# Order of the first loads, split first weights, idle products at the start, GpSimd adds between the layers, and last tiles by token halves

## The chip, the cores and the metric

The kernel runs on one core of one Trainium2 chip. The metric is the device time of one execution in microseconds (us); the time before is the median of three runs.

## The reference

Two transformer-like blocks are applied to 512 tokens of width 1024, everything in float32. The first block is a mixer of three branches and an MLP; the second has two layers of three sub-blocks each. Cut to what matters here:

```python
# first block
u = rms_norm(x, g_mix); z = u @ w_in              # the first product is the slice "v" of w_in
...                                               # three branches, merge, h = h + y @ w_o, MLP
h = rms_norm(h, g_final)
# second block, for each layer l of 2
def post_add(x, y, i, res_w):
    return x + res_w * mod[:, i, 2] * rms_norm(y, norm_post[l, i])
x = post_add(x, swiglu(pre(x, 0), ffn_w_in[l, 0], ffn_w_out[l, 0]), 0, 0.5)
x = post_add(x, token_mixer(pre(x, 1), ...), 1, 1.0)
x = post_add(x, swiglu(pre(x, 2), ffn_w_in[l, 1], ffn_w_out[l, 1]), 2, 0.5)
```

`pre` is an RMS norm with a scale and a shift for each feature. Both norms need, for each token, a sum of squares over all 1024 features, which lie on partitions and in 8 tiles.

## The kernel before, in words

A tensor of 1024 features by 512 tokens is held as 8 tiles of 128 partitions x 512 tokens: `hT` is the running state, `Y` (`YT`) the output of a sub-block, `XH` and `XL` the normed input as a high and a low part. Every float32 product is made of three: high weights by high input, low weights by high input, and high weights by low input. ScalarE rounds a weight block to its high part (`hi`, L1339: `wh<-w`), VectorE subtracts it to get the low part (`lo`, L2024: `wl<-w,wh`). All weights come through three slots of 1 MB (`wslots`), loaded by SyncE in the order of the stages (`load` inside the `sync` block, L496). A block's slot is free (`w_free`) once its `lo` is done. `plan` lists the stages, their blocks `s.b`, their output tiles `s.o`, the PSUM bank of each, and which `hi`/`lo` of a later block is done ahead of which tile (`s.ahead`).

The order of each engine's work is written out by hand, engine by engine; each instruction counts up its engine's semaphore, and `at(name)` is the count another engine waits for.

The start: SyncE issues four pieces of x (each 2 tiles, 512 KB), the constants `cf`, the parameters `pr`, the bf16 constants (`BIG<-in_cb`), and then weight blocks. ScalarE squares the 8 tiles of x (L1405), VectorE adds them in a tree (L1976), TensorE sums over partitions by products with a constant column (`token_sums`, L725), ScalarE takes the root (L1371), VectorE the reciprocal, and TensorE spreads the four columns of factors over a PSUM bank (`spread`, L752). VectorE then makes the normed tile k (`feed`, L2066), ScalarE its high part (`high`, L1401), and TensorE starts stage `v` (`four_tiles`, L610): for each k, 8 products of 128x512 on four output tiles; the 32 products with `XL` follow. Product k=4 needs the second weight block of `v`.

The links: after a sub-block, `link` forms both norms at once. TensorE makes the sums and two spreads, then 8 idle products (`warm`, L732). VectorE then goes through the tiles in a pipeline: `scaled(k)` (L2490, Y times gain and factor, the factor in PSUM bank 4), `added(k)` (L2496, hT = hT + Y, all in SBUF), `normed(k)` (L2502, the next norm, its factor in PSUM bank 2). ScalarE makes `XH` of tile k (L1703), and TensorE takes it in `four_tiles` (L610 or L612). Five links have such an addition; the link from the first block (`final`) has none. Where the next stage is `u` (two links), VectorE also makes the low part of a weight block in two halves (`lo_half`, L2032), the second one ahead of the wait for the first spread.

GpSimd (`POOL`) has the sums of the dots (`y_adds`, L3016) and low parts in the FFNs (L2998). It is idle in the part of the link described.

The end: the last stage is `("out", 3, 2)` with four weight blocks of two output tiles each, 6 x 3 products of 128x512 a tile. VectorE adds a finished tile to `Y` (L2780), ScalarE squares it (L1722), GpSimd gathers. After the last tile, `last_link` (TensorE) and `last_post` (VectorE) make the norm and the last addition: 8 times `scaled` (L2525) and 8 times `added` (L2529), and SyncE stores a tile of `hT` as soon as it is done (L545).

Of the kernel before, what the change touches and what calls it, by code (L numbers as in the profile page):

```python
# [9 lines left out]
F32 = mybir.dt.float32  # L10
# [13 lines left out]
CF = {}  # L24
# [54 lines left out]


# [53 lines left out]
_T = [("j", 0)] * 3  # L134

# [108 lines left out]
def program(nc, A, out, marks_in):  # L244
# [4 lines left out]
    with ctx:  # L249
# [54 lines left out]
        x_landed = [sem(f"x_landed{i}") for i in range(4)]  # L304
        const_landed, w2_landed, rg_landed, mem_landed, xo_landed, c_landed = [sem(n) for n in (
# [29 lines left out]
        def last_mm(name):  # L335
            return at("mm", st_of[name].o[-1][-1])

# [145 lines left out]
        def _(sp):  # L483
            for i in range(4):
                sp.dma_start(hT[:, 2 * i:2 * i + 2, :], A["x"].rearrange("p (k t) -> p k t", k=8)[:, 2 * i:2 * i + 2]).then_inc(
                    x_landed[i], 16)
            sp.dma_start(cf[:, :], A["cf"]).then_inc(const_landed, 16)
            sp.dma_start(pr[:, :], A["pr"]).then_inc(const_landed, 16)
            sp.dma_start(BIG[:, 0:NCB], A["cb"]).then_inc(const_landed, 16)
            ticks, mod_end = 0, MOD_FIRST  # L490

            def load(s, g):
                b = s.b[g]
                if b >= 3:
# [48 lines left out]
            for k in range(8):  # L543
                sp.wait_ge(*at("h_new", (1, 2), k))
                sp.dma_start(out[:, 512 * k:512 * k + 512], hT[:, k, :]).then_inc(out_landed, 16)  # L545
            sp.wait_ge(*at("bar", "end", "dve"))
            sp.wait_ge(*at("bar", "end", "pool"))
            sp.wait_ge(out_landed, 128)

        @block.tensor  # L550
        def _(pe):
# [50 lines left out]
            def four_tiles(s, xh, xl, xw):  # L602
# [13 lines left out]
                for k in range(8):  # L616
                    pe.wait_ge(*xw("h", k))
                    for t in range(4):
                        if (k, t) == (0, 0):
                            pe.wait_ge(*at("lo", s.b[0]))  # L620
# [25 lines left out]
            def gemm(s, xh, xl=None, xw=None):  # L646
# [7 lines left out]
                for g, b in enumerate(s.b):  # L654
                    if s.four and g < 2:
                        continue
                    if s.raw:
# [57 lines left out]

            def run(s, xh, xl=None, xw=None, after=None):
# [54 lines left out]
            run(st_of["v"], XH, XL, xw("mix"))  # L771
            run(st_of["g"], XH, XL)
# [320 lines left out]
            def last_link(r):  # L1093
                pe.wait_ge(*at("y_acc", r))
                token_sums(banks[3], tmps[4], 512, True, False)
                pe.wait_ge(*at("y_sq", r, 7))
                token_sums(banks[3], tmps[2], 512, False, True).then_inc(*TE.up(("sq_mm", ("y", r), 7)))
                warm(3)
                spread(("y", r), 512)

            def ffn(l, f):
# [15 lines left out]
                if r == (1, 2):  # L1117
                    last_link(r)
# [208 lines left out]
        def _(act):  # L1327
# [22 lines left out]
            def evict(s, fn, ahead=True):  # L1350
                for g, b in enumerate(s.b):
                    for t, o in enumerate(s.o[g]):
# [50 lines left out]
            for k in range(8):  # L1403
                act.wait_ge(x_landed[k // 2], 16)
                actf(tmps[k][:, :], hT[:, k, :], ACT.Square).then_inc(*AC.up(("sq", "mix", k)))  # L1405
            act.wait_ge(const_landed, 48)
            first_root()
            root("mix", 512)
            hi(st_of["v"], 0)
# [304 lines left out]
            def last_square(r, j, wait):  # L1714

                t = tmps[4] if j == 0 else tmps[2] if j == 7 else tmps[j % 2]
# [3 lines left out]
                if 3 <= j < 7:  # L1720
                    act.wait_ge(*at("y_add", r, j - 2))
                actf(t[:, :], Y[:, j, :], ACT.Square).then_inc(*AC.up(("y_sq", r, j)))  # L1722

# [62 lines left out]
            def ffn(l, f):  # L1786
# [30 lines left out]
                if r == (1, 2):  # L1817
                    root(("y", r), 512)
# [142 lines left out]
        def _(dve):  # L1961
# [8 lines left out]
            for m in (1, 2, 4):  # L1970
                for k in range(0, 8, 2 * m):
                    if m == 1:
                        dve.wait_ge(*at("sq", "mix", k + 1))
                    elif k == 0:
                        own()
                    tt(tmps[k][:, :], tmps[k][:, :], tmps[k + m][:, :], ALU.add).then_inc(*DV.up(("x_sq",)))  # L1976
            dve.wait_ge(const_landed, 48)
            v.tensor_copy(cb_[:, :], BIG[:, 0:NCB]).then_inc(*DV.up(("cb",)))
# [56 lines left out]
            def evict(s, fn, ahead=True):  # L2035
                for g, b in enumerate(s.b):
                    for t, o in enumerate(s.o[g]):
# [47 lines left out]
            lo(st_of["v"], 0)  # L2085
            dve.wait_ge(*at("spread", "mix"))
            feed("mix", lambda k: p("g_mix", k), norm_low("mix"), HIGH_FIRST[0:4])
            lo(st_of["v"], 1)
            feed("mix", lambda k: p("g_mix", k), norm_low("mix"), HIGH_FIRST[4:8] + [("l", k) for k in LOWS])
            run(st_of["v"])  # L2090
# [358 lines left out]
            def link(r, nxt):  # L2449
# [31 lines left out]
                if nxt[1] == 1:  # L2481
                    lo_half(st_of[("u", nxt[0])], 1, 1)
# [10 lines left out]
                def added(k):  # L2493
                    if not final:
                        dve.wait_ge(*at("y_scaled", r, k))
                        tt(hT[:, k, :], hT[:, k, :], Y[:, k, :], ALU.add).then_inc(*DV.up(("h_new", r, k)))  # L2496

# [9 lines left out]
                added(0)  # L2507
                for k in range(8):
# [3 lines left out]
                    if k < 7:  # L2512
                        added(k + 1)
# [6 lines left out]
            def last_post(r):  # L2520
                gc = newc(168)
                rms(("y", r), 512)
                for k in range(9):
                    if k < 8:
# [732 lines left out]
```

## Time and profile before

| what | us |
|---|---|
| median of 3 runs (3423.95 to 3426.64) | 3424.88 |
| the profiled execution's own time | 3428.77 |
| its span | 3427.0 |
| TensorE busy (PE, 98%) | 3352.0 |
| VectorE busy (DVE, 49%) | 1673.1 |
| ScalarE busy (ACT, 36%) | 1224.2 |
| GpSimd busy (POOL, 13%) | 435.4 |

The profile has engines in columns: PE is TensorE's products, PEld its weight loads, DVE VectorE, ACT ScalarE, POOL GpSimd, SP SyncE. A float32 product that isn't of the rounded kind shows as two records. "L705" is a line of the kernel; the arrow points from inputs to the output tile.

### The profile page before, as it was taken

What the parts mean: (1) busy time and instruction counts of PE and PEld (TensorE: products, weight loads), DVE (VectorE), ACT (ScalarE), POOL (GpSimd) and SP (SyncE); (2) the same over time, 40 slices, a digit from 0 to 9 for tenths busy, and PEclk for the clock granted to TensorE, in tenths of its full rate; (3) what the DMA queues carried; (4) which work ended last, traced back from release to release, by engine and by line L of the source; (5) the groups of instructions that cost most, each with busy time, mean ns of one, the idle gap of its engine ahead of it and who ended that gap; (6) DMA issues with size and microseconds to landing.
All of it is one profiled execution on the core that took longest, in us unless ns stands there. A gap on an engine that the chain in (4) does not pass through costs nothing.

```text
span 3427.0 us, 38703 instructions
## 1 busy us (share of the span) xinstructions
PE 3352.0 (98%) x16102; PEld 2640.4 (77%) x16110; DVE 1673.1 (49%) x2190; ACT 1224.2 (36%) x1770; POOL 435.4 (13%) x338
## 2 busy tenths in 40 slices
PE   8999999999999999999999999999999999999998
PEld 6755477788888888888588888878888876888886
DVE  5555666453335635664335534575457533452233
ACT  3374466332223232224533322233223245342222
POOL 0100013122220100112011100110101210210001
PEclk9999999999999999999999999999999999999999
DMA  5412643243333333223032344433431322222221
GB/s 192 148 44 81 185 172 131 109 148 142 140 143 119 107 138 137 75 111 117 21 121 99 135 143 146 135 115 111 152 105 68 124 92 68 86 86 99 99 95 53
DMA packets 78351, 393.40 MB, mean 115 GB/s; under 512 B 8416, under 2 KB 17120, under 8 KB 45024
## 3 DMA queue, kind: packets, MB, share of 16 engines
q1 hardware_dynamic: 66048, 370.41, 30.9%
q10 hardware_dynamic: 12128, 20.52, 1.7%
q8 instruction: 127, 2.08, 0.2%
q14 instruction: 48, 0.39, 0.0%
HBM read 372.02 MB, written 18.87 MB: 114 GB/s over the span
## 4 chain that ended last, share of the span: by engine, by line
PE 91%; DVE 4%; ACT 3%; issue 2%; DMA 0%; ACTq 0%; POOL 0%; SPq 0%; DVEq 0%; POOLq 0%
PE pb L705 22%; PE pb L707 21%; PE pb L706 21%; PE pb L612 3%; PE pb L673 2%; PE pb L674 2%; PE pb L610 2%; PE pb L681 2%; PE pb L876 1%; PE pb L894 1%; PE pb L855 1%; ACT wh L1339 1%; DVE wl L2024 1%; PE pb L1211 1%; PE pb L1161 1%
## 5 line engine op out<-in xcount | busy, mean ns | idle before, releaser
L2024 DVE TENSOR_TENSOR wl<-w,wh 128x2048 fp32r<-128x2048 f32 (+3 forms) x264 | 582.8, 2207 | 889.0 <-ACT wh L1339 886.6
L705 PE MATMUL pb<-XH,wh 128*128 128x512 f32 (+1 forms) x2488 | 985.0, 396 | 2.4 <-DVE wl L2024 1.6
L707 PE MATMUL pb<-XH,wl 128*128 128x512 f32 (+1 forms) x2488 | 970.9, 390 | 0.0
L706 PE MATMUL pb<-XL,wh 128*128 128x512 f32 (+1 forms) x2488 | 970.1, 390 | 0.0
L1339 ACT ACTIVATE wh<-w 128x2048 fp32r<-128x2048 f32 (+3 forms) x264 | 471.7, 1787 | 284.5 <-PE pb L707 188.3
L705 PEld LDWEIGHTS pb<-XH,wh 128*128 128x128 f32 (+1 forms) x2488 | 466.5, 188 | 108.6 <-issue 8.2
L706 PEld LDWEIGHTS pb<-XL,wh 128*128 128x128 f32 (+1 forms) x2488 | 466.5, 187 | 101.7 <-issue 4.6
L707 PEld LDWEIGHTS pb<-XH,wl 128*128 128x128 f32 (+1 forms) x2488 | 465.9, 187 | 100.9
L2998 POOL TENSOR_TENSOR HL<-tmps,HH 128x512 fp32r<-128x512 f32 x120 | 165.6, 1383 | 1312.3 <-ACT HH L1661 1312.3
L705 PE MATMUL pb<-HH,wh 128*128 128x512 f32 x768 | 303.0, 394 | 2.3 <-DVE YT L2780 2.3
L706 PE MATMUL pb<-HL,wh 128*128 128x512 f32 x768 | 301.1, 392 | 0.0
L707 PE MATMUL pb<-HH,wl 128*128 128x512 f32 x768 | 301.1, 392 | 0.0
L2011 DVE CUSTOM_DVE_ANT_0 mreg<-mreg,pr 128x1024 f32<-128x1024 f32 x144 | 187.1, 1300 | 39.0 <-DMA mreg<-in_mod_w 38.8
L1661 ACT ACTIVATE HH<-tmps 128x512 fp32r<-128x512 f32 x120 | 75.4, 631 | 347.9 <-DVE tmps L2771 329.9
L705 PEld LDWEIGHTS pb<-HH,wh 128*128 128x128 f32 x768 | 145.9, 190 | 33.7 <-DVE YT L2780 3.7
L707 PEld LDWEIGHTS pb<-HH,wl 128*128 128x128 f32 x768 | 145.6, 190 | 30.8
L706 PEld LDWEIGHTS pb<-HL,wh 128*128 128x128 f32 x768 | 145.9, 190 | 30.1
L1797 ACT ACTIVATE tmps<-pb 128x512 f32<-128x512 f32 x88 | 52.4, 598 | 307.5 <-PE pb L707 281.7
L2771 DVE TENSOR_TENSOR tmps<-tmps,pb 128x512 f32<-128x512 f32 x88 | 60.3, 687 | 185.6 <-PE pb L707 181.4
L673 PE MATMUL pb<-HH,wh 128*128 128x512 f32 x256 | 99.6, 389 | 0.0
L674 PE MATMUL pb<-HH,wl 128*128 128x512 f32 x256 | 99.6, 389 | 0.0
L2780 DVE TENSOR_TENSOR YT<-YT,pb 128x512 f32<-128x512 f32 x64 | 43.8, 685 | 111.7 <-PE pb L707 86.0
(479 smaller groups left out, 4057.8 us busy)
## 6 DMA issues: line engine op xcount, KB each, us to landing
w<-in_f_in SPq DMA_DIRECT2D x88, 1024.0 KB, 4.8
mreg<-in_mod_w SPq DMA_DIRECT2D x144, 512.0 KB, 3.6
w<-in_f_out SPq DMA_DIRECT2D x32, 1024.0 KB, 5.0
w<-in_w_up SPq DMA_DIRECT2D x16, 1024.0 KB, 5.7
w<-in_w_dn SPq DMA_DIRECT2D x16, 1024.0 KB, 5.7
w<-in_m_g SPq DMA_DIRECT2D x16, 1024.0 KB, 4.8
w<-in_f_out SPq DMA_DIRECT2D x16, 768.0 KB, 4.2
w<-in_w_rm SPq DMA_DIRECT2D x8, 1024.0 KB, 5.7
```

The lines of the kernel that those rows point to most:

```text
L610: return mm(dst, tokens(s, x, k, t), slot(s, k // 4)[part][:, 512 * (k % 4):512 * (k % 4) + 512], **kw)
L612: return mm(dst, slot(s, t // 2)[part][:, at_:at_ + 128], x[:, k, :], **kw)
L673: mm(dst, hi[:, cs], xh[:, k, :], start=k == 0, stop=False)
L674: mm(dst, lo[:, cs], xh[:, k, :], start=False, stop=False)
L705: mm(dst, hi[:, cs], xh[:, k, :], start=k == 0, stop=False)
L706: mm(dst, hi[:, cs], xl[:, k, :], start=False, stop=False)
L707: x = mm(dst, lo[:, cs], xh[:, k, :], start=False, stop=fin)
L1339: actf(slot(s, g)[0][:, 0:s.cols], wslots[b % 3][:, 0:s.cols], ACT.Copy).then_inc(*AC.up(("hi", b)))
L1661: actf(HH[:, j, :], t, ACT.Copy).then_inc(*AC.up(("hh", *name, j)))
L2011: v.tensor_tensor_reduce(out=mslots[t % 2], in0=mslots[t % 2], in1=csil, scale=1.0, scalar=p("mod_b", t), op0=ALU.mult, op1=ALU.add, accum ...
L2024: tt(low[:, 0:s.cols], wslots[b % 3][:, 0:s.cols], h[:, 0:s.cols].bitcast(F32), ALU.subtract).then_inc(*DV.up(("lo", b), ("w_free", b)))
L2998: tt(HL[:, j, :], t, HH[:, j, :].bitcast(F32), ALU.subtract).then_inc(*PO.up(("hl", *name, j)))
```

## The change

What it does, in five parts; the diff is cut to the code that carries them.

1. Loads and first weights. The constants `cf` are loaded in three pieces: the identity (128 columns) and the last 17 columns after the first piece of x, the middle one (1409 columns) with the bf16 constants behind the second weight block. The first weight block of `v` comes in two halves of 512 KB with semaphores of their own, ahead of `pr`; ScalarE and VectorE split it half by half. `four_tiles` waits for the first half at k=0 and for the whole at k=2.
2. First norm. ScalarE takes a root of a dummy first and squares 7 tiles, VectorE squares the eighth. The tree is replaced by three groups (tiles 0-3, 4-5, 6-7), each summed over tokens by its own four products.
3. Idle products. GpSimd clears `cb_` at once; TensorE runs 24 idle products of 128x512 on it, then waits for the constants and the first sums.
4. Links. The additions k = 1 to 7 go to GpSimd (`h_adds`), k = 0 stays; the second `lo_half` moves behind `normed(1)` and `scaled(3)`.
5. End. Output tiles 4 to 7 of the last stage are computed for tokens 0-255 and then for tokens 256-511 (`half_tiles`), 144 products of 128x256 in place of 72 of 128x512. Sums, root, reciprocal, spread, scaling, addition and store follow for each half, the first half's sums and spread between the products of the second; additions are shared by VectorE and GpSimd. There are 16 stores in place of 8.

```diff
@@ sync
+            front, tail = CF["ropeC"][0], CF["padmax"][0]
             for i in range(4):
                 sp.dma_start(hT[:, 2 * i:2 * i + 2, :], ...).then_inc(x_landed[i], 16)
-            sp.dma_start(cf[:, :], A["cf"]).then_inc(const_landed, 16)
-            sp.dma_start(pr[:, :], A["pr"]).then_inc(const_landed, 16)
-            sp.dma_start(BIG[:, 0:NCB], A["cb"]).then_inc(const_landed, 16)
+                if i == 0:
+                    sp.dma_start(cf[:, 0:front], A["cf"][:, 0:front]).then_inc(first_landed, 16)
+                    sp.dma_start(cf[:, tail:NCF], A["cf"][:, tail:NCF]).then_inc(first_landed, 16)
...
+                if b == 0:
+                    sp.dma_start(wslots[0][:, 0:1024], s.srcs[0][:, 0:1024]).then_inc(half_landed, 16)
+                    sp.dma_start(wslots[0][:, 1024:2048], s.srcs[0][:, 1024:2048]).then_inc(w_landed[0], 16)
+                    sp.dma_start(pr[:, :], A["pr"]).then_inc(pr_landed, 16)
+                    return
...
+                if b == 1:
+                    sp.dma_start(cf[:, front:tail], A["cf"][:, front:tail]).then_inc(const_landed, 16)
+                    sp.dma_start(BIG[:, 0:NCB], A["cb"]).then_inc(const_landed, 16)
@@ tensor
+            def half_tiles(s, xh, xl, between):
+                for n, (half, j) in enumerate(HALF_TILES):       # (0,4..7), (1,4..7)
+                    g, t = j // 2, j % 2
+                    if half == 0 and t == 0:
+                        pe.wait_ge(*at("lo", s.b[g]))
+                    if n < 2:
+                        bank_free(s, s.o[g][t])
+                    else:
+                        pe.wait_ge(*at("ev_half", s.name, *HALF_TILES[n - 2]))
+                    for k in range(kts):                          # three products of 128x256
...
+                        if (half, j, k) in between:
+                            between[half, j, k]()
...
-            pe.wait_ge(const_landed, 48)
-            pe.wait_ge(*at("x_sq"))
-            token_sums(banks[3], tmps[0], 512, True, True).then_inc(*TE.up(("sq_mm", "mix", 7)))
+            pe.wait_ge(*at("cb_zero"))
+            warm(24)
+            pe.wait_ge(first_landed, 32)
+            pe.wait_ge(*at("x_sum", 3))
+            token_sums(banks[3], tmps[0], 512, True, False)
+            pe.wait_ge(*at("x_sum", 5))
+            token_sums(banks[3], tmps[4], 512, False, False)
+            pe.wait_ge(*at("x_sum", 7))
+            token_sums(banks[3], tmps[6], 512, False, True).then_inc(*TE.up(("sq_mm", "mix", 7)))
...
-                    last_link(r)
+                    half_tiles(st_of[("out", i, 2)], HH, HL, {(1, 4, 3): lambda: last_sums(r, 0), (1, 5, 1): lambda: last_spread(0)})
+                    last_sums(r, 1)
+                    warm(2)
+                    last_spread(1)
@@ vector, link
-                if nxt[1] == 1:
-                    lo_half(st_of[("u", nxt[0])], 1, 1)
                 dve.wait_ge(*at("spread", name))
...
                 for k in range(8):
                     normed(k)
                     if k < 6:
                         scaled(k + 2)
-                    if k < 7:
-                        added(k + 1)
+                    if k == 1 and nxt[1] == 1:
+                        lo_half(st_of[("u", nxt[0])], 1, 1)
@@ vector, last_post
+                for j in range(4, 8):
+                    add_y(0, j)
+                add_y(1, 4)
+                inverse(0)
+                dve.wait_ge(*at("last_spread", 0))
+                scaled(0, 0, 1, 2)
+                add_y(1, 5)
+                scaled(0, 3, 4)
+                added(0, 3)
+                add_y(1, 6)
+                scaled(0, 5, 6, 7)
+                added(0, 4)
+                add_y(1, 7)
+                inverse(1)
+                dve.wait_ge(*at("last_spread", 1))
+                scaled(1, 0, 1)
+                for k in (2, 4, 6):
+                    scaled(1, k)
+                    added(1, k - 1)
+                    scaled(1, k + 1)
+                added(1, 7)
@@ gpsimd
+            gp.memset(cb_[:, :], 0.0).then_inc(*PO.up(("cb_zero",)))
...
+            def h_adds(r):
+                for k in range(1, 8):
+                    pool.wait_ge(*at("y_scaled", r, k))
+                    tt(hT[:, k, :], hT[:, k, :], Y[:, k, :], ALU.add).then_inc(*PO.up(("h_new", r, k)))
+            # last_adds: gathered(0, 4..6), gathered(1, 4), added(0, 0), gathered(1, 5), added(0, 1, 2),
+            #            gathered(1, 6), added(0, 5, 6, 7), added(1, 0, 2, 4, 6)
```

## Rows read from the trace of the kernel before

**Rows 1.** The profile's first lines: span, and busy time of TensorE's products and others.

```profile
span 3427.0 us, 38703 instructions
PE 3352.0 (98%) x16102; PEld 2640.4 (77%) x16110; DVE 1673.1 (49%) x2190; ACT 1224.2 (36%) x1770; POOL 435.4 (13%) x338
```

**Rows 2.** Timeline, first 45 us: start, duration, engine, line, operation, count [idle before].

```profile
7.50 2.43 ACT L1405 ACTIVATE tmps<-hT 128x512 f32<-128x512 f32 x4 [0.44 <-DMA hT<-in_x]
12.86 1.83 PE L725 MATMUL pb<-cf,tmps 128*128 128x1 f32 x8 [12.86 <-DVE tmps L1976]
15.26 2.08 PE L752 MATMUL pb<-cf,rcol 128*128 128x128 f32 x8 [0.56 <-DVE rcol L2084]
20.70 0.80 PE L610 MATMUL pb<-wh,XH 128*128 128x512 f32 x1 [3.36 <-ACT XH L1401]
22.53 1.90 ACT L1339 ACTIVATE wh<-w 128x2048 fp32r<-128x2048 f32 x1
24.46 2.29 DVE L2024 TENSOR_TENSOR wl<-w,wh 128x2048 fp32r<-128x2048 f32 x1 [2.50 <-ACT wh L1339]
26.78 2.72 DVE L2066 SCALAR_TENSOR_TENSOR tmps<-hT,pr,pb 128x512 f32<-128x512 f32 x4
37.13 7.42 PE L610 MATMUL pb<-wh,XL 128*128 128x512 f32 x32
```

**Rows 3.** Busy time by stretch: stretch, PE, PEld, DVE, ACT, POOL (records), granted clock, DMA.

```profile
20.70:24.20 3.50, 3.50 (x8) 2.82 (x9) 1.26 (x2) 3.45 (x4) 0.00 (x0) 1.00 0.92 379
1871.30:1873.00 1.70, 1.70 (x9) 1.70 (x9) 0.52 (x4) 0.30 (x1) 0.00 (x0) 0.50 0.96 402
```

**Rows 4.** DMA issues of the first 40 us: KB each, median us to landing.

```profile
BIG<-in_cb SPq DMA_DIRECT2D x1, 256.0 KB, 8.3
```

**Rows 5.** Timeline of one link into an FFN, VectorE and TensorE.

```profile
1875.15 0.75 DVE L2502 SCALAR_TENSOR_TENSOR tmps<-hT,cols,pb 128x512 f32<-128x512 f32 x1
1877.20 0.75 DVE L2502 SCALAR_TENSOR_TENSOR tmps<-hT,cols,pb 128x512 f32<-128x512 f32 x1
1876.97 0.47 PE L612 MATMUL pb<-XH,wh_extra 128*128 128x512 f32 x1 [0.53 <-ACT XH L1703]
1892.76 0.62 PE L612 MATMUL pb<-XL,wh_extra 128*128 128x512 f32 x2
```

**Rows 6.** Timeline of one link into stage `u`.

```profile
1465.94 1.20 DVE L2032 TENSOR_TENSOR wl<-w,wh 128x1024 fp32r<-128x1024 f32 x1
1470.97 0.60 PE L610 MATMUL pb<-wh,XH 128*128 128x512 f32 x1 [0.77 <-ACT XH L1703]
1486.97 7.68 PE L610 MATMUL pb<-wh,XL 128*128 128x512 f32 x32
```

**Rows 7.** Timeline of GpSimd and of VectorE beside it, at two places.

```profile
1508.40 1.30 POOL L3045 TENSOR_TENSOR tmps<-tmps 128x512 f32<-128x512 f32 x1 [20.63 <-DVE tmps L2819]
1508.77 0.68 DVE L2821 TENSOR_TENSOR tmps<-pb,BIG 128x512 f32<-128x512 f32 x1
2238.51 1.28 DVE L2011 CUSTOM_DVE_ANT_0 mreg<-mreg,pr 128x1024 f32<-128x1024 f32 x1
2238.67 2.25 POOL L3016 TENSOR_TENSOR tmps<-tmps 128x512 f32<-128x512 f32 x1 [5.36 <-DVE tmps L2446]
```

**Rows 8.** Timeline of TensorE in the compression products (two records to a product).

```profile
158.76 5.19 PE L811 MATMUL pb<-tmps,w 128*128 128x124 f32 x45
```

**Rows 9.** Timeline of the end.

```profile
3394.95 1.76 DVE L2024 TENSOR_TENSOR wl<-w,wh 128x1536 fp32r<-128x1536 f32 x1 [2.08 <-ACT wh L1339]
3408.08 0.39 PE L707 MATMUL pb<-HH,wl 128*128 128x512 f32 x1
3409.91 1.29 PE L725 MATMUL pb<-cf,tmps 128*128 128x1 f32 x8 [0.66 <-ACT tmps L1722]
3412.29 1.87 PE L752 MATMUL pb<-cf,rcol 128*128 128x128 f32 x8
3423.09 1.29 DVE L2529 TENSOR_TENSOR hT<-hT,YT 128x512 f32<-128x512 f32 x2
```

More of the change, by code:

```diff
@@ L134 @@
 _T = [("j", 0)] * 3
+HALF_TILES = [(half, j) for half in range(2) for j in range(4, 8)]
 def _steps(what, a, b):
@@ L336, in last_mm, with hs, half_bank @@
             return at("mm", st_of[name].o[-1][-1])
+        def hs(half):
+            return slice(256 * half, 256 * half + 256)
+        def half_bank(s, n):
+            return banks[s.bank[s.o[2][n % 2]]]
         def newc(i, n=8):
@@ L619, in four_tiles @@
                         if (k, t) == (0, 0):
+                            pe.wait_ge(*at("lo_half" if s.name == "v" else "lo", s.b[0]))
+                        if (k, t) == (2, 0) and s.name == "v":
                             pe.wait_ge(*at("lo", s.b[0]))
@@ L1817, in ffn @@
                 if r == (1, 2):
-                    root(("y", r), 512)
+                    for more in st_of[("out", i, 2)].ahead[2, 0]:
+                        hi(*more)
+                    for half, j in HALF_TILES:
+                        last_half(r, j, half)
+                        if (half, j) == (1, 4):
+                            last_root(0)
+                    last_root(1)
                 else:
@@ L2506, in link @@
                 scaled(1)
-                added(0)
+                if not final:
+                    dve.wait_ge(*at("y_scaled", r, 0))
+                    tt(hT[:, 0, :], hT[:, 0, :], Y[:, 0, :], ALU.add).then_inc(*DV.up(("h_new", r, 0)))
                 for k in range(8):
@@ new lines, in add_y, with inverse @@
+                def add_y(half, j):
+                    dve.wait_ge(*at("mm_half", st_last.name, half, j))
+                    tt(Y[:, j, hs(half)], Y[:, j, hs(half)], half_bank(st_last, j)[:, hs(half)], ALU.add).then_inc(
+                        *DV.up(("ev_half", st_last.name, half, j)))
+                def inverse(half):
+                    cs = slice(2 * half, 2 * half + 2)
+                    dve.wait_ge(*at("last_root", half))
+                    v.reciprocal(rcol[:, cs], rcol[:, cs]).then_inc(*DV.up(("last_inverse", half)))
@@ new lines, in scaled, with added @@
+                def scaled(half, *ks):
+                    for k in ks:
+                        stt(out=Y[:, k, hs(half)], in0=Y[:, k, hs(half)], scalar=gc[:, k:k + 1], in1=banks[4][:, hs(half)],
+                            op0=ALU.mult, op1=ALU.mult).then_inc(*DV.up(("y_scaled", r, k, half)))
+                def added(half, *ks):
+                    for k in ks:
+                        dve.wait_ge(*at("y_scaled", r, k, half))
+                        tt(hT[:, k, hs(half)], hT[:, k, hs(half)], Y[:, k, hs(half)], ALU.add).then_inc(
+                            *DV.up(("h_new", r, k, half)))
@@ new lines, in last_post @@
+                for more in st_last.ahead[2, 0]:
+                    lo(*more)
+                for j in range(4, 8):
+                    add_y(0, j)
+                own()
+                add_y(1, 4)
[8 more added lines that the diff above has]
+                added(0, 4)
@@ L3062, in _ @@
                 y_adds(r)
+                h_adds(r)
                 ffn(l, 1)
```

169 lines of the change are left out of this document (123 added, 46 removed).

## The prediction

> **What bounds the kernel now.** Read the first lines first: TensorE's products fill 3352 of 3427 us [rows 1]. So nothing that only relieves another engine can pay; what is left are the 75 us in which TensorE has no product, and products that run at the lower clock. The waits by engine say where: 12.9 us before the first sum, 3.4 us before the first product of stage `v`, about 1 us inside each link, and the timeline shows some 18 us behind the last product. The change touches just these, so each is worked out from its timeline, as a chain: what is the last thing that its end waits for. Sums are made in the profiled execution (its own time 3428.77, span 3427.0), which is 3.9 above the median of 3424.88; I carry the difference over to the median.
>
> **The start.** The chain before: last piece of x there at about 8.7 (the last two squares end at 9.93, 0.62 each), the tree of adds, eight records of sums from 12.86 to 14.7, root and reciprocal until 15.26, spread until 17.3, low part of the first block on VectorE until 19.2, normed tile and high part, first product 20.70; the `XL` products start at 37.13 [rows 2]. TensorE and VectorE both stood in front of the constants too: the last of them landed at 3.71 + 8.3 = 12.0 [rows 4].
>
> After, step by step. The two small pieces of `cf` go ahead of x's second to fourth piece. By bytes that is 73 KB at the 3.45 MB that had landed by 12.0, 0.2 us; I take 0.4 and keep 1.2 as the upper end, for 256 short descriptors and two more issues in SP's queue. The last x is there at 9.1. ScalarE squares 7 of 8 and VectorE the eighth; then one add: the last group is ready at 11.1 (an add is 0.69 long and they follow at 0.60, [rows 9]; the second group's add, from 9.1, and VectorE's square stand in front of it). Four products of sums: 0.9 at the full clock (as the 1.29 and less of [rows 9] tell, partly slow), 1.83 at the low one [rows 2]; I take 1.4, to 12.5. Root, reciprocal and their gaps took 15.26 - 14.69 = 0.6: 13.1. Spread 0.9 to 2.08; I take 1.7: 14.8. In its shadow go the first half of `hi` (about 1.0 of 1.90) before the root, and half of `lo` (1.20, [rows 6]) between reciprocal and spread. `pr` has about as many bytes in front of it as before the last constant, so 12.2: hidden. Normed tile 0.7 and high part 0.65 and the first product starts at 16.2, 4.5 earlier.
>
> But the gain is not read there. Product k=4 wants the second weight block, whose `hi` stands behind `high(3)` on ScalarE and whose `lo` stands ahead of `normed(4)` on VectorE. That chain: 14.8, two normed tiles 1.35, half a `lo` 1.2, two normed tiles 1.35, high part 0.7, `hi` 1.90, `lo` 2.29, normed tile 0.7, high part 0.7 [rows 2]: 25.1. TensorE, with 32 products at 0.227, would be there at 23.5, or at 25.2 if 8 of them run at the low clock (3.5 us for 8, [rows 3]). So an early clock is worth little here: at 25.1 VectorE's chain takes the place of the clock. Before, k=4 began at 37.13 - 32 x 0.227 = 29.9 (from the pace inside the 7.42 of [rows 2]). Gain 4.8 at most, I take 4.7. With everything at the full clock it is 5.6; with sums and spread at the low clock and the loads late, 3.
>
> The 24 idle products (about 8 slow ones at 0.43, then 16 fast ones at 0.22) end between 8 and 10, so they are over before the last group is ready. Their good is the clock of sums and spread, 0.9 and 0.8 us, and that is not sure: in a link the granted clock was at half (0.50, the 1.2 GHz level) from 1871.3, after a stretch in which TensorE had run small products and hardly a wide one [rows 3]; here it runs nothing and then small products between the idle ones and the spread. That is why I took the middle for the sums and nearly the low clock for the spread. The moved cast, `cf`'s middle and the bf16 constants are wanted only after `v`: they land near 17, the `v` stage ends near 39. Later stages are TensorE's, so the 4.7 stay.
>
> **The links.** VectorE's pace for a tile is 1877.20 - 1875.15 = 2.05 (three operations); TensorE needs 8 products, 1.85 at 0.231 (an estimate between the 0.227 of [rows 2] and the 0.235 of [rows 6]). The 64 products went from 1876.97 to 1892.76, 15.8 in place of 14.75: 1.04 of waits [rows 5]. After, VectorE has two operations, 1.35, and GpSimd one of 1.30; both below 1.85. GpSimd's k=1 starts with `scaled(1)`, when `added(0)` does, and ends 1.35 later, before `normed(1)` is due. The first product can't come earlier: `normed(0)` is unchanged. Gain 1.0 for each of three links. In the two links into `u` the products took 16.0 for 64 x 0.235 = 15.04 (the pace inside the 7.68), 0.96 [rows 6]. The `lo_half` that stood ahead of the first `scaled` and ended at 1467.14 gives something between nothing and the 0.77 idle in front of the first product; I take 0.45. It now stands between `scaled(3)` and `normed(2)`, which delays tile 2 by 1.2; TensorE has it near 0.25 late. 1.15 each. Sum: 3 x 1.0 + 2 x 1.15 = 5.3.
>
> What may go wrong is seen in [rows 7]. GpSimd's add took its 1.30 beside VectorE's operation with one input in PSUM, and 2.25 where VectorE ran operations with both inputs in SBUF. In the link, `scaled` and `normed` read PSUM, so I take 1.30; only `lo_half` and, at the end, `added` have both in SBUF. The Trainium skill (GPSIMD Engine Reference, its opening paragraphs) calls this engine the wrong choice for ordinary elementwise arithmetic, since VectorE is about twice as fast. The ratio fits the 1.30 against 0.69 here, and by that rule alone the seven adds would cost 7 x 0.6 = 4.2 more in each link; the sum above says that they do not, because they stand beside.
>
> **The end.** Before: last product starts 3408.08, sums of the last tile from 3409.91, spread ends 3414.16, then eight pairs of `scaled` and `added` to 3424.38, and 2.6 for the last store [rows 9]. After, from the end of tile 3 (3408.3 less 72 x 0.226, 3392.1): 144 products of 256 columns. Their pace is nowhere in the trace. Half of 0.2133 (512 columns at 2.4 GHz) and the same 0.0133 on top make 0.120. A weight load goes with each; in the compression stage a record with its own 128x128 load came every (5.19 - 0.275)/44 = 0.112 [rows 8], so a load fits. Below 0.112 I see no way; upward 0.227, as if nothing were halved. I take 0.120, nearest to rows 8.
>
> Half tiles 2.16 each: tiles 4 and 5 done at 3396.4. Tile 6 needs the low part of block 3 (until 3396.7) and the bank of tile 4, which VectorE adds behind that: 3397.2, a stall of 0.8. Then 3401.5 for the first half. In the second half come sums (0.9) and spread (0.45) of the first; for the spread TensorE waits 0.7 for root and reciprocal, as ScalarE takes the root behind the square of (1, 4). Last product ends at 3412.2, 3.7 later than before. Then add 0.4, square 0.4, two products of sums 0.45, root and reciprocal 0.55, spread 0.45 to 0.9: 3414.9. On VectorE 8 `scaled` of 256 columns (0.385: half of the 0.55 that grows with size, and 0.11) and 4 `added` (0.35) make 4.5, and 0.4 of waits on GpSimd, which has five adds of 0.7; the first half is scaled and stored by then. 3419.8; plus 2.6 gives 3422.4. Gain 4.6; I take 4.5.
>
> **Sum.** 4.7 + 5.3 + 4.5 = 14.5: 3424.9 - 14.5 = 3410.4. A second place where a rule is weighed: the Trainium skill (DMA: Bandwidth & Descriptors, Specifications) wants at least 512 B in a transfer, below which engines read and modify; the 17 columns of the tail are 68 B a row. No row here prices it, and by it I would only move to the upper end of 1.2 on the loads, 0.8 less gain.
>
> **The rivals.**
> A (chance 0.78): the forecast.
> B, VectorE and GpSimd disturb each other in the links (0.08). If each add takes 2.25 as in rows 7, it is GpSimd's pace that counts, 2.3 a tile against 2.05: 7 x 0.25 = 1.75 more in each of five links, +8.8 in place of -5.3; 3424.5. Against it: the 1.30 beside a PSUM operand.
> C, half products with a pace between, 0.16 (0.06): 144 x 0.04 = 5.8 more; 3416.2.
> D, the weight load isn't hidden behind a product of half the length (0.04). Load and product in a row, the load's own record being 0.19 long and the product 0.12, make 0.31 each: 144 x 0.19 = 27 more, 3437. It decides from 0.120 + 14.5/144 = 0.221 on. For it: the load's record is longer than the product. Against it: rows 8, where the record is as long too.
> E, the start doesn't move, since the loads and not the order set it (0.04): no 4.7; 3415.1.
>
> **How the numbers follow.** The likeliest gives 3410.4; its own uncertainty is 1.7 at the start, 1.5 in the links, and 2.5 at the end (each 0.01 in pace is 1.4). C and E lie within some 6 of it, B and D outside. 3405.5 to 3416.5. About 0.2% (6.8 us) can be told from no change: faster 0.91 (A, C, E and a part of the rest), same 0.06 (B), slower 0.03 (D).
>
> **What would show it.** After: `L610` starts near 16 and the `XL` products near 32.5; a wait of TensorE before k=4 of `v`, released by ScalarE's `XH`. In links, GpSimd's adds of 1.3 and no wait inside the 64 products. Half products at 0.120, a last product near 3412 minus the 10 gained before it, and last `added` about 7.5 behind it. Wrong if half products come at over 0.14, if GpSimd's adds are 1.6 or more in the links, or if the gain at `v` is lost before stage `g`.

## The result and the profile after

| | us |
|---|---|
| before, median of 5 runs | 3424.88 (3423.95 to 3426.91) |
| after, median of 5 runs | 3411.97 (3409.83 to 3414.70) |
| ratio, 95% interval | 0.9956 (0.9945 to 0.9967) |
| after, the profiled execution's own time / span | 3411.97 / 3410.2 |

The change saves 12.9 us. The forecast was 3410.4.

The first lines of the profile after, to be read against [rows 1]:

```profile
span 3410.2 us, 38986 instructions
PE 3354.3 (98%) x16221; PEld 2644.4 (78%) x16221; DVE 1650.0 (48%) x2167; ACT 1223.1 (36%) x1774; POOL 492.6 (14%) x387
```

TensorE's busy time rose by 2.3 us, the idle products included. Its time without a product fell from 75.0 to 55.9, and that makes the 16.8 us by which the span is shorter. GpSimd has 57 us more: some 49 for the adds in the links and 8 for those at the end.

**The start after**, timeline, same columns as [rows 2]:

```profile
4.77 1.15 ACT L1482 ACTIVATE tmps<-hT 128x512 f32<-128x512 f32 x2 [2.53 <-DMA hT<-in_x]
8.11 1.15 ACT L1482 ACTIVATE tmps<-hT 128x512 f32<-128x512 f32 x2 [2.20 <-DMA hT<-in_x]
9.76 1.86 ACT L1482 ACTIVATE tmps<-hT 128x512 f32<-128x512 f32 x3 [0.50 <-DMA hT<-in_x]
10.86 4.74 PE L778 MATMUL pb<-cf,tmps 128*128 128x1 f32 x24 [2.59 <-DVE tmps L2076]
12.35 0.69 DVE L2083 TENSOR_TENSOR tmps<-tmps 128x512 f32<-128x512 f32 x1
16.23 2.08 PE L805 MATMUL pb<-cf,rcol 128*128 128x128 f32 x8 [0.63 <-DVE rcol L2191]
19.87 0.79 PE L635 MATMUL pb<-wh,XH 128*128 128x512 f32 x1 [1.56 <-ACT XH L1476]
36.92 7.42 PE L635 MATMUL pb<-wh,XL 128*128 128x512 f32 x32
```

The first sum starts 2 us earlier than in [rows 2], yet the spread starts 1 us later and the first product only 0.8 earlier. Two things stand out: ScalarE waits 2.20 us for the second piece of x, and 24 records of sums take 4.74 us. The `XL` products start at 36.92, against 37.13. So in this execution almost nothing was gained at the start.

**A link into an FFN after**, VectorE, GpSimd and TensorE, against [rows 5]:

```profile
1873.44 0.75 DVE L2612 SCALAR_TENSOR_TENSOR tmps<-hT,cols,pb 128x512 f32<-128x512 f32 x1
1876.25 0.75 DVE L2612 SCALAR_TENSOR_TENSOR tmps<-hT,cols,pb 128x512 f32<-128x512 f32 x1
1877.59 0.75 DVE L2612 SCALAR_TENSOR_TENSOR tmps<-hT,cols,pb 128x512 f32<-128x512 f32 x1
1880.41 0.75 DVE L2612 SCALAR_TENSOR_TENSOR tmps<-hT,cols,pb 128x512 f32<-128x512 f32 x1 [0.60 <-POOL hT L3204]
1870.01 1.65 POOL L3204 TENSOR_TENSOR hT<-hT,YT 128x512 f32<-128x512 f32 x1 [15.32 <-DVE YT L2605]
1872.11 2.62 POOL L3204 TENSOR_TENSOR hT<-hT,YT 128x512 f32<-128x512 f32 x2 [0.46 <-DVE YT L2605]
1872.44 0.50 PE L637 MATMUL pb<-XH,wh_extra 128*128 128x512 f32 x1
1887.11 0.62 PE L637 MATMUL pb<-XL,wh_extra 128*128 128x512 f32 x2
```

VectorE needs 1.34 from the tile at 1876.25 to the next, where it needed 2.05. Over the five tiles from 1873.44 to 1880.41 it is 1.39, since it waits a little for GpSimd, whose adds take 1.31 each beside it and follow each other at 1.4. The first add, which runs beside VectorE's own, takes 1.65. The 64 products of this link take 14.67, where [rows 5] had 15.79.

**The end after**, against [rows 9]:

```profile
3379.50 0.28 PE L761 MATMUL pb<-HH,wh 128*128 128x256 f32 x1
3379.61 0.28 PE L762 MATMUL pb<-HL,wh 128*128 128x256 f32 x1
3379.73 0.28 PE L763 MATMUL pb<-HH,wl 128*128 128x256 f32 x1
3379.85 0.28 PE L761 MATMUL pb<-HH,wh 128*128 128x256 f32 x1
3400.06 0.61 PE L1156 MATMUL pb<-cf,tmps 128*128 128x1 f32 x4
3401.12 0.61 PE L1160 MATMUL pb<-cf,tmps 128*128 128x1 f32 x4 [0.46 <-ACT tmps L1811]
3402.28 0.71 PE L1167 MATMUL pb<-cf,rcol 128*128 128x128 f32 x4
3403.03 1.26 DVE L2647 SCALAR_TENSOR_TENSOR YT<-YT,cols,pb 128x256 f32<-128x256 f32 x3 [0.80 <-PE pb L1167]
```

The half products follow each other at 0.120 (24 of them from 3379.50 to 3382.37). From the first of them to the end of the span are 30.7 us; from the same point, the end of tile 3, it was 35.0 before.

### The profile page after: what moved, and what is told of

Its sections match the earlier page's. It is cut to its first block, busy times and chain, and to the rows that moved or that the text cites. A ratio compares the mean times of both kernels' runs of the same rounds, so it can differ in the third digit from the quotient of the medians.

```text
span 3410.2 us, 38986 instructions
## 1 busy us (share of the span) xinstructions
PE 3354.3 (98%) x16221; PEld 2644.4 (78%) x16221; DVE 1650.0 (48%) x2167; ACT 1223.1 (36%) x1774; POOL 492.6 (14%) x387
## 4 chain that ended last, share of the span: by engine, by line
PE 91%; DVE 4%; ACT 2%; issue 2%; DMA 0%; POOL 0%; SPq 0%; ACTq 0%; DVEq 0%; POOLq 0%
PE pb L734 22%; PE pb L736 21%; PE pb L735 21%; PE pb L637 3%; PE pb L702 2%; PE pb L703 2%; PE pb L635 2%; PE pb L710 2%; PE pb L936 1%; PE pb L954 1%; PE pb L915 1%; ACT wh L1412 1%; PE pb L1284 1%; DVE wl L2129 1%; PE pb L1234 1%
## 5 line engine op out<-in xcount | busy, mean ns | idle before, releaser
L2129 DVE TENSOR_TENSOR wl<-w,wh 128x2048 fp32r<-128x2048 f32 (+2 forms) x263 | 580.3, 2206 | 888.0 <-ACT wh L1412 885.7
L1412 ACT ACTIVATE wh<-w 128x2048 fp32r<-128x2048 f32 (+2 forms) x263 | 469.7, 1786 | 287.3 <-PE pb L736 188.4
L734 PE MATMUL pb<-HH,wh 128*128 128x512 f32 x744 | 291.3, 391 | 2.3 <-DVE YT L2931 2.3
L736 PE MATMUL pb<-HH,wl 128*128 128x512 f32 x744 | 290.3, 390 | 0.0
L735 PE MATMUL pb<-HL,wh 128*128 128x512 f32 x744 | 290.2, 390 | 0.0
L734 PEld LDWEIGHTS pb<-HH,wh 128*128 128x128 f32 x744 | 140.2, 188 | 32.5 <-DVE YT L2931 3.7
L702 PE MATMUL pb<-HH,wh 128*128 128x512 f32 x256 | 99.6, 389 | 0.0
L703 PE MATMUL pb<-HH,wl 128*128 128x512 f32 x256 | 99.6, 389 | 0.0
```

Source lines behind the costliest of these rows:

```text
L702: mm(dst, hi[:, cs], xh[:, k, :], start=k == 0, stop=False)
L703: mm(dst, lo[:, cs], xh[:, k, :], start=False, stop=False)
L734: mm(dst, hi[:, cs], xh[:, k, :], start=k == 0, stop=False)
L735: mm(dst, hi[:, cs], xl[:, k, :], start=False, stop=False)
L736: x = mm(dst, lo[:, cs], xh[:, k, :], start=False, stop=fin)
L1412: actf(slot(s, g)[0][:, 0:s.cols], wslots[b % 3][:, 0:s.cols], ACT.Copy).then_inc(*AC.up(("hi", b)))
```

## The experiments

Each number below is a median against the runs of the kernel before on the same chip (3425.8 to 3426.5).

**The three parts alone, and the whole again.** `start_only` has the first loads, the halved first weight block, the three groups of sums and the idle products. `links_only` is this, and `end_only` the rest of the diff:

```
@@ links_only, VectorE and GpSimd
-                if nxt[1] == 1:
-                    lo_half(st_of[("u", nxt[0])], 1, 1)
...
-                    if k < 7:
-                        added(k + 1)
+                    if k == 1 and nxt[1] == 1:
+                        lo_half(st_of[("u", nxt[0])], 1, 1)
...
+                for k in range(1, 8):
+                    pool.wait_ge(*at("y_scaled", r, k))
+                    tt(hT[:, k, :], hT[:, k, :], Y[:, k, :], ALU.add).then_inc(*PO.up(("h_new", r, k)))
```

> The kernel before with the new start alone (load order, split first weights, three groups of sums, 24 idle products); links and end as before. Theory T, from the trace of the changed kernel: the start gave almost nothing (the XL products of stage v start at 36.92, 0.2 earlier), because the small pieces of the constants delay x by about 2 us and the sums, the spread and 12 products run at the low clock. Then 3424.0 to 3425.5, profile: XL products of v between 36 and 38. Rival R1, the prediction's step: the start is worth 4.7 and the profiled run was an odd one: 3420.2, XL products near 32.5.

> The kernel before with GpSimd's additions in the five links and the moved half of the low part; start and end as before. T: 5.3 us from the waits inside the 64 products and the half low part, so 3419.6, give or take 1.7 for each stretch at the low clock that falls more or less often (before: two in each link). Rival R2: the 12 us gained between the start and the last stage belong to the links as such: 3413 or less.

> The kernel before with the last four output tiles by token halves; start and links as before. T: 3392.0 to 3427.0 was 35.0 us behind tile 3, the changed kernel has 30.7: 4.3 gained, 3420.6. Rival R3: the end also took the clock's stretches elsewhere with it, or its 4.3 depend on the rest: more than 6, or less than 3.

> The changed kernel once more, with a new profile. T: 3412 again with a spread of some 5 us, wider than the 3 of the kernel before, and the stretches of granted half clock (13 after the start in the first profile, 16 before) fall in other places and in another number, each worth 1.7. Rival R2: the places and the number are the same.

| kernel | median (runs) | us less than before | ratio, interval |
|---|---|---|---|
| start_only | 3423.52 (11) | 2.7 | 0.9993 (0.9984 to 1.0001) |
| links_only | 3418.61 (10) | 7.6 | 0.9978 (0.9968 to 0.9987) |
| end_only | 3422.15 (11) | 4.0 | 0.9989 (0.9980 to 0.9998) |
| after_again | 3415.25 (5) | 10.9 | 0.9967 (0.9955 to 0.9980) |

The parts add up to 14.3, and the whole gave 12.9 and 10.9: no sign that they disturb each other beyond the noise. The end came as predicted, the links brought more than 5.3, and the start less than 4.7. The interval of the start reaches nought, so its size is read from its trace: there the `XL` products start at 34.92, 2.2 earlier. That lies between what was expected before the run (36 to 38) and its rival (32.5), so neither was right.

**The small pieces behind x.** `x_first`:

```
-                if i == 0:
+                if i == 3:
                     sp.dma_start(cf[:, 0:front], A["cf"][:, 0:front]).then_inc(first_landed, 16)
```

> The changed kernel with the two small pieces of the constants issued behind all four pieces of x in place of behind the first. T: they are what slowed the loads (three profiles with the new start moved 340 GB/s or less until x was there, those with the old one 400), the last squares end near 9.9 as before in place of 10.7 to 11.6, and the first product comes 1 us earlier than in the two profiles of the changed kernel (17.8 and 19.9): near 16.8. Time 1 less than the changed kernel, hardly told apart by rounds. Rival R4: two descriptors' worth of small rows cost little; the slower rate has to do with more issues in the queue, and nothing moves.

3410.26 (5 runs, 3407.72 to 3415.92), ratio 0.9956 (0.9944 to 0.9969). The last square of ScalarE and the sums in its timeline:

```profile
8.77 0.63 ACT L1482 ACTIVATE tmps<-hT 128x512 f32<-128x512 f32 x1 [0.23 <-DMA hT<-in_x]
9.17 3.51 PE L778 MATMUL pb<-cf,tmps 128*128 128x1 f32 x24 [1.03 <-DMA cf<-in_cf]
```

ScalarE has its last piece of x at 8.77, as the kernel before had (near 8.7), where `after` was still busy with three squares from 9.76 on; the last group is ready at 10.72 against 13.04. This is more than one odd execution. With the pieces ahead, the last group was ready at 12.15 (`start_only`), 12.47 (`after_again`), 12.93 (`no_idle`, below) and 13.04; with them behind, at 10.72 and, in the two kernels further below, at 10.91 and 10.55.

Part of it is the issuing itself. These lines are SyncE's queue (SPq), two of `after` and then one of `x_first`:

```profile
1.17 0.42 SPq L503 DMA_DIRECT2D cf<-in_cf  x1
2.11 1.38 SPq L500 DMA_DIRECT2D hT<-in_x  x3
```

```profile
0.74 1.80 SPq L500 DMA_DIRECT2D hT<-in_x  x4
```

Each issue takes 0.38 to 0.43 and a gap, so the two extra ones bring the last piece of x into the queue at 3.06 in place of 2.11, 0.95 later. From its issue to its landing it then took 7.9 in place of 6.6. Issue and landing together make nearly all of the 2.3. The rates show the second share. These lines are the DMA's GB/s in 40 slices of the first 12 us, first `after`, then `x_first`:

```profile
GB/s 0 0 0 0 0 82 82 96 259 273 423 348 323 159 195 221 287 314 341 273 178 191 164 178 259 218 287 341 382 410 410 437 369 396 423 423 396 428 420 449
```

```profile
GB/s 0 0 0 0 0 82 96 96 246 314 355 382 423 437 423 369 328 396 396 410 382 423 423 396 372 337 353 413 411 369 246 246 287 355 382 399 425 447 484 455
```

In `after` the rate is at 159 to 341 from 3.9 to 8.4. The two pieces of `cf` had landed by 4.3 and 5.1, so they share the engines with x only in the first part of that stretch; what held the rate down behind them is not shown. In `x_first` the pieces have landed by 9.2, and a shorter dip to 246 comes at 9, behind x. So their place in the order cost the last group 2.3 us in that execution, not the 0.2 that their bytes make. `x_first` moves the issues and the short rows together, and so it doesn't separate the two; the rival R4 (more issues in the queue) holds for up to 0.95 of it. Now the sums wait for `cf` (1.03 us), which is cheap. How much the pieces cost differs from one execution to the next: with the same order of loads the first sum started at 9.40 in `start_only` and at 10.61 in `after_again`.

**Without the idle products.** `no_idle` is the changed kernel without `warm(24)`.

> The changed kernel without the 24 idle products at the start. T: they end at 8.3 to 9.6 and the clock falls within the sums, so without them sums (24 records) run at the low clock throughout, 5.5 in place of 3.0 to 4.7, first product 1 to 2 later; low clock in v as without. Time 0 to 2 more. Rival R5: the idle products carry the gain at the start: 3 or more slower, XL products of v near 38.

3414.48 (5 runs), ratio 0.9968 (0.9955 to 0.9980): 12.0 less than before, which can't be told from the 12.9 and 10.9 with the idle products. The trace says more. Its sums, spread and first product:

```profile
10.23 5.25 PE L778 MATMUL pb<-cf,tmps 128*128 128x1 f32 x24 [10.23 <-DVE tmps L2075]
16.11 2.08 PE L805 MATMUL pb<-cf,rcol 128*128 128x128 f32 x8 [0.63 <-DVE rcol L2190]
19.75 0.80 PE L635 MATMUL pb<-wh,XH 128*128 128x512 f32 x1 [1.56 <-ACT XH L1475]
```

A record of sums takes 0.22 throughout, so 24 of them form a queue of 5.25 us. In `start_only`, where the clock held until 13.1, each group of eight took 1.02 to 1.10 and was over before the next was ready; in `after` the clock fell at 11.4 and stayed at half until 25.1. What counts is the time from the moment when the last group is ready to the end of the sums: 2.55 in `no_idle` (12.93 to 15.48), 2.56 in `after` (13.04 to 15.60), 1.11 in `after_again` and 1.16 in `start_only`. The idle products thus brought nothing in `after` and 1.4 in the other two, one execution each. In line with that, the `XL` products start at 36.46 in `no_idle`, no later than the 36.92 of `after`, and at 33.98 in `after_again`. Their effect ends before the spread: that took 2.07 or 2.08 in each of these traces.

**Idle products between the groups.** `x_first_bridge`:

```
+            warm(4)
             pe.wait_ge(*at("x_sum", 5))
...
+            warm(3)
             pe.wait_ge(*at("x_sum", 7))
...
+            warm(3)
             spread("mix", 512)
```

> As x_first, and with 4, 3 and 3 more idle products between the groups of sums and before the spread. T: they fill gaps in which TensorE waits, the clock stays at full for sums and spread, 0.9 each in place of up to 1.9 and 2.1; first product near 15.5, but then the second weight block's chain on ScalarE and VectorE sets k=4: XL products of v near 32.5 in place of 34 to 37. Time 2 less than the changed kernel. Rival R6: the idle products stand in front of the sums and delay them, no gain.

3409.26 (5 runs, 3407.95 to 3414.98), ratio 0.9956 (0.9943 to 0.9970). Busy time of TensorE in three stretches (sums, spread, first products), first `after`, then `x_first_bridge`; the third column from the end is the granted clock:

```profile
10.86:15.60 4.74, 4.74 (x24) 4.66 (x24) 1.99 (x3) 1.74 (x3) 0.00 (x0) 0.56 1.03 428
15.60:18.30 2.70, 2.07 (x9) 1.78 (x8) 1.29 (x2) 1.21 (x2) 0.00 (x0) 0.50 1.00 391
19.87:25.00 5.13, 5.13 (x12) 4.07 (x13) 2.60 (x4) 3.61 (x4) 0.15 (x1) 0.50 0.87 305
```

```profile
9.30:14.10 4.80, 4.77 (x34) 3.58 (x34) 1.70 (x5) 1.80 (x4) 0.00 (x0) 1.00 0.99 401
14.10:16.80 2.70, 1.20 (x9) 0.97 (x8) 2.56 (x4) 1.34 (x3) 0.00 (x0) 1.00 1.00 406
16.86:21.00 4.14, 4.14 (x18) 3.45 (x19) 2.43 (x3) 2.83 (x4) 0.78 (x2) 1.00 1.06 407
```

With the bridges the clock stays at its full level (1.00, 2.4 GHz), the spread takes 1.16, and 18 first products take 4.14, where 12 took 5.13. But the first product comes at 16.86, not near the expected 15.5, and hardly earlier than the 16.95 of `x_first`: the bridges stand in the same queue as the sums, which end 2.6 behind the moment when the last group is ready (10.91 to 13.51; 1.96 in `x_first`), and three more idle products stand in front of the spread, so that the shorter spread only makes up for them. Rival R6 is right on this point. What the bridges bring is the full clock of the first products, and there the wait that the prediction named shows up. The `XL` products start at 33.05 (33.68 in `x_first`), which is 16.2 behind the first product, where 64 products at 0.227 are 14.5. The weight block's chain:

```profile
19.89 1.90 ACT L1415 ACTIVATE wh<-w 128x2048 fp32r<-128x2048 f32 x1
21.83 2.29 DVE L2132 TENSOR_TENSOR wl<-w,wh 128x2048 fp32r<-128x2048 f32 x1 [2.51 <-ACT wh L1415]
24.16 2.72 DVE L2176 SCALAR_TENSOR_TENSOR tmps<-hT,pr,pb 128x512 f32<-128x512 f32 x4
24.94 2.61 ACT L1479 ACTIVATE XH<-tmps 128x512 fp32r<-128x512 f32 x4 [3.14 <-DVE tmps L2176]
```

VectorE sits idle for 2.51 us until ScalarE's cast is done, and k=4 starts at 25.62, behind a wait of 1.21. The prediction had 25.1 for this.

**The cast earlier.** `hi_early` is `x_first_bridge` with one line changed:

```
                 high("mix", k, tmps[k][:, :], XH)
-                if k == 3:
+                if k == 1:
                     hi(st_of["v"], 1)
```

> x_first_bridge with one line moved: the cast of the second weight block of v stands on ScalarE behind the second high part (k=1), not the fourth (k=3). In x_first_bridge VectorE sat idle for 2.5 us until that cast (19.89 to 21.8) was done, and TensorE waited 1.2 us in front of k=4. Theory T (the wait in front of k=4 is the chain cast, low part, normed tile, high part that the prediction named): the cast runs from about 17.4 to 19.3, low part 19.4 to 21.7, normed tile 4 until 22.4, its high part until 23.1, TensorE is due there at 24.1 by 32 products of 0.227 from 16.86: no wait, the XL products start near 31.8 (33.05 before), whole time 1.2 less than x_first_bridge, 3408. Rival R (something else sets k=4, as the landing of the block, or high parts 2 and 3, which now come behind the cast, become the bound): XL stays at 33 or later, and there is a wait of TensorE in front of k=2 or k=3.

```profile
16.77 0.50 PE L635 MATMUL pb<-wh,XH 128*128 128x512 f32 x1 [1.56 <-ACT XH L1479]
31.41 7.41 PE L635 MATMUL pb<-wh,XL 128*128 128x512 f32 x32
```

64 products in 14.64 with no wait left: T is right to 0.4 us, and the `XL` products start 5.7 earlier than in the kernel before. In the whole time it can't be told from its neighbours, and the 1.2 less that T expected doesn't show: 3410.25 (6 runs, 3400.48 to 3418.51), ratio 0.9954 (0.9941 to 0.9967).

**The links' two edits apart.** `links_adds` and `links_half` each take one half of the diff shown for `links_only`.

> Only the seven adds of each of the five links go to GpSimd; the half low part stays where it stood, ahead of the first scaled tile. links_only (adds and moved half) gave 7.6 us less than before by the medians, with an interval of about 3.4, where the prediction's sum for the links was 5.3. Theory T (the prediction's terms): 1.0 in each of five links, 5.0 less; the 64 products of a link take 14.7 to 14.9 in place of 15.8 to 16.0; GpSimd's adds 1.30 to 1.4. Rival R (most of the gain is the moved half, which lets scaled(0) start earlier in two links): adds alone give 3 or less.

> Only the half low part of the second weight block is moved in the two links into u, from ahead of the first scaled tile to behind scaled(3); VectorE keeps all its adds. Theory T (the prediction's terms): the first product comes up to 0.77 earlier but tile 2 is 1.2 later, with VectorE as the bound of the link's tiles: between 0.5 less and 1 more, the median unchanged within 0.1%. Rival R (the missing 2.3 us of links_only are here): 2 us less. In the profile: time from the reciprocal to the first product in links into u, and the length of the 64 products behind it (16.0 before).

`links_adds` 3422.26 (11 runs), ratio 0.9991 (0.9983 to 1.0000); `links_half` 3428.02 (11 runs), ratio 1.0001 (0.9992 to 1.0010). By these times alone neither T nor R could be refuted for `links_adds`: 3.5 less, with an interval from nought to some 6. The timelines of the first link into `u` tell more, in us:

```
                     last product before the link    64 products,
                     to first product after it       until XL
before               10.34                           16.00
links_adds           10.34                           15.24
links_half            9.28                           16.99
links_only            9.28                           15.24
after                 9.27                           15.24
```

In none of these five does a stretch at half clock fall into the 64 products. So the moved half takes 1.06 off the way to the first product, since `scaled(0)` starts right behind the reciprocal. VectorE alone gives all but 0.07 of it back inside the 64 products, with a wait of 0.72 in front of tile 2. Beside GpSimd's adds it gives nothing back. These are the first product, and that wait, of `links_half`:

```profile
1468.63 0.59 PE L610 MATMUL pb<-wh,XH 128*128 128x512 f32 x1 [0.95 <-ACT XH L1703]
1473.47 0.63 PE L610 MATMUL pb<-wh,XH 128*128 128x512 f32 x1 [0.72 <-ACT XH L1703]
```

R is refuted by these rows: neither half alone holds the extra gain, the two together do. In a link into an FFN the 64 products went from 15.8 to 14.6 with the adds, five links in sum 3 x 1.18 + 2 x (0.76 + 1.06) = 7.2, in fair agreement with the 7.6 timed. That `links_adds` shows 3.5 in place of the 5.1 that its rows make lies inside its interval.

**Why the totals scatter.** Each trace has stretches, 3.4 us long or twice that, in which the granted clock is at half. Most lie at the links, where TensorE runs small products and waits: in `before`, 12 of 16 begin between 16.3 us ahead of the first product behind a link and 1.5 behind it. Which link gets two of them, one or none changes from execution to execution. A product takes 0.427 in them instead of 0.227, so that nearly half their length is lost where TensorE is busy. Added up over the span without its first and last 30 us, and half of it taken off the span:

```
                 span     at half clock   span less half of it
before           3427.0   54.6            3399.7
start_only       3421.9   51.2            3396.3
links_only       3418.2   54.6            3390.9
links_adds       3417.0   41.0            3396.5
links_half       3426.2   54.6            3398.9
end_only         3423.7   51.2            3398.1
after            3410.2   44.4            3388.0
after_again      3408.1   41.0            3387.6
no_idle          3412.6   44.4            3390.5
x_first          3414.1   58.0            3385.1
x_first_bridge   3406.2   44.4            3384.0
hi_early         3408.3   47.8            3384.4
```

In the last column the two executions of the changed kernel agree to 0.4, and 11.7 and 12.1 are the gain; the span's 16.8 held 5.1 of luck with the clock. The column is rough all the same. It gives 8.8 for `links_only` and 3.2 for `links_adds`, where their rows make 7.2 and 5.1, and 1.6 for `end_only`, where the trace has 4.3. By this column `x_first` and `x_first_bridge` are 3 to 4 us better than the change, which is hardly more than its error. Timed, they are 16.2 and 17.2 below before, `hi_early` 15.5, against 12.9 and 10.9 for the change, with intervals that overlap. They are the best versions found; that they beat the change is likely, not shown. Nor is it shown whether the change makes the stretches rarer: their sum is 41.0 to 58.0 with the adds on GpSimd and 51.2 to 54.6 without.

## Why the prediction was right, and where it was not

- **What bounds the kernel**: held. The whole gain is idle time of TensorE, in the three places named.
- **The end**: 4.5 predicted, 4.3 in the trace (35.0 to 30.7), 4.0 timed. The pace of half products, the one size no row showed, was 0.120 as taken. From the first half product to the end of the last 20.6 were measured and 20.1 predicted; from there to the end of the span 10.1, with 10.2 predicted. Rival C (0.16) and rival D (a weight load that isn't hidden) are refuted by the spacing of L761 to L763.
- **The links**: mechanism right, size 5.3 against 7.2. The mis-sized term is the moved half of the low part: I took 0.45 of its 0.77 and then charged tile 2 with 0.25, where it gives 1.06 and costs nothing. Of the terms for the products, 1.0 for an FFN link was 1.18, and 0.96 for a link into `u` was 0.76. Rival B fell: of 35 adds the median is 1.30 and the longest are 2.2, the two that run beside the low part of the weights with both inputs in SBUF, as [rows 7] had let expect. So GpSimd's pace is 1.4 a tile and stays below the 1.85 of TensorE, though not below VectorE's 1.35.
- **The start**: 4.7 predicted; 0.2, 3.2 and 2.2 in three traces (`after`, `after_again`, `start_only`), 2.7 timed for the start alone. Two steps failed. The first is "I take 0.4 and keep 1.2 as the upper end": the small pieces made the last group later by 2.3 us in `after` and some 1.4 in `start_only` (ready at 12.15, against 10.72 in `x_first`). Of this 0.95 is the later issue of the last piece of x, and the rest its longer way to landing. The Trainium skill (DMA: Bandwidth & Descriptors, Specifications) wants at least 512 B in a transfer for the full rate. The identity's rows have just that, the tail's 68 B lie below, and no run here separates the two; the rate was at 159 to 221 GB/s from 3.9 to 4.8, while such pieces ran, which agrees in direction, but it was as low again from 6.0 to 7.2, when they had landed. The second step is "four products of sums: 0.9 at the full clock, I take 1.4", which priced the last group alone, but at the low clock the three groups queue: 24 records of 0.22 need 5.2 us, more than the 2.2 us from the first group to the last. In `after` the first product came 3.7 later than predicted: 1.9 by the late last group, 1.2 by the queue of sums behind it, 0.6 by the slow spread and what followed. The `XL` products came 4.4 later than the 32.5 predicted: these 3.7, and 0.7 more because 12 first products ran at the low clock, where the prediction had room for 8.
- **The idle products**: "their good is the clock of sums and spread, 0.9 and 0.8 us" held for the spread in no trace (2.07 or 2.08 each time), and for the sums in two of three.
- **k=4 of `v`**: the claim that VectorE's chain takes the place of the clock was not reached in `after`, where TensorE was late enough to hide it. With the clock repaired it appeared at 25.6 (25.1 predicted), and went when its first link was moved.
- **Rival E**, the start doesn't move, had a chance of 0.04, which was too low: one execution of three shows it, and the loads, which it named, are a part of the reason.

The total came out within 1.6 us because the start was 2 too large and the links 1.9 too small; the 1.6 itself lies inside the noise, as `after_again` with 10.9 shows. The sign and the range rested on the terms that held; the closeness of the middle is luck.

## What to carry over

Small loads that go ahead of a large one are not to be priced by their bytes: count the time of their issues and look at when the large one lands; put them behind what the first work waits for. Split a reduction into groups only where a group is over before the next is ready, at the clock that really holds there. Idle wide products between the groups can keep the clock, but they stand in the same queue and delay what is behind them. Two edits on one engine's queue can be worth more together than apart: a wait moved behind tiles costs nothing only once something else has been taken off that queue.

## What the runs showed of the hardware

- 24 idle products of 512 columns did not hold TensorE's clock through the small products behind them: over at 8.3, it was at half from 11.4 in `after`; over at 9.6, from 14.1 in `after_again`. Four, three and three more between the groups kept it at full without a break (spread 1.16 in place of 2.08).
- The profile's granted clock can't be read before its first change: in `no_idle` no record is at half in the first 30 us, while a record of sums took 0.22 instead of 0.11, and [rows 3] give 1.00 with eight products in 3.5 us.
- Stretches at half clock, 3.4 us long or twice that: 11 to 16 in a span without its first and last 30 us, most of them at the links, about 1.7 us lost for each 3.4. The mean granted clock of a run goes with its time: in `hi_early` 3400.48 at 0.995, 3408.54 to 3410.41 at 0.992, 3413.13 at 0.991 and 3418.51 at 0.989.
- SyncE issues a DMA every 0.47 us (from 1.17 to 1.64 and to 2.11 in `after`), so two small loads ahead of a large one put it off by 0.95 before a byte is moved.
- GpSimd's add of 128x512 takes 1.30 while VectorE reads PSUM, and 1.65 to 2.2 where VectorE has both inputs in SBUF. VectorE's add of 128x256 took 0.85 and 0.77 twice at the end beside GpSimd's adds of the same kind, but 0.41 to 0.44 four times in the second half, where GpSimd was adding as well; what makes the difference is not shown.
